# Input normalised with tokens on partitions and then transposed, parameter rows moved behind the first weight panel

## The reference

```python
def rms_norm(x, g):
    y = xf * lax.rsqrt(jnp.mean(xf * xf, axis=-1, keepdims=True) + RMS_EPS)
    return (y * g.astype(jnp.float32)).astype(x.dtype)

h = h + token_mixer(rms_norm(h, g_mix[l]), w_in[l], rnn_conv_w[l], ...)
    # inside: z = u @ w_in; split into u_rnn, u_gelu, c_val, c_gate, z_ga, z_gb
    # RG-LRU branch on u_rnn/u_gelu, 31-tap causal convolution branch on c_val/c_gate,
    # merged by sigmoid gates and projected by w_out
h = h + hierarchical_moe(rms_norm(h, g_ffn[l]), ...)
return rms_norm(h, g_final)
```

## Time and profile before

| | us |
|---|---|
| Median of 3 runs | 533.61 (533.55 to 533.82) |
| Span of the profiled execution | 531.7 |
| The profiled execution's own device time | not listed |
| TensorE busy in it | 509.5 (96%) |
| VectorE, ScalarE, GpSimd busy | 273.2, 209.2, 9.6 |
| Mean granted TensorE clock | 0.987 |

### The profile page before, as it was taken

How to read it: one execution, slowest core, us unless ns; L and a number is a source line. 1 busy time by engine, 2 the same in 40 slices (tenths; PEclk the granted TensorE clock), 3 DMA queues, 4 the chain that set the end, 5 groups by cost and what they waited for, 6 DMA issues and landing times.

```text
span 531.7 us, 8105 instructions
## 1 busy us (share of the span) xinstructions
PE 509.5 (96%) x2983; PEld 359.7 (68%) x2983; DVE 273.2 (51%) x550; ACT 209.2 (39%) x315; POOL 9.6 (2%) x25
## 2 busy tenths in 40 slices
PE   4999999999999999999989999999999999999994
PEld 4998888888999999999964353535435353534531
DVE  0589999969999996678282202221221212122123
ACT  2561113323897779345243231412323141322414
POOL 3020000000000000000000000000000000000000
PEclk8799999999999999999999999999999999999998
DMA  7594995434444438759996999999999999999932
GB/s 238 171 250 159 300 301 182 141 125 146 152 154 163 158 109 283 244 166 326 322 387 248 363 361 373 372 350 369 356 367 372 372 361 359 372 372 369 355 137 79
DMA packets 115970, 143.31 MB, mean 270 GB/s; under 512 B 3934, under 2 KB 106398, under 8 KB 115946
## 3 DMA queue, kind: packets, MB, share of 16 engines
q1 hardware_dynamic: 115502, 141.75, 79.5%
q0 software_dynamic: 432, 1.21, 0.8%
q10 hardware_dynamic: 12, 0.02, 0.0%
HBM read 141.90 MB, written 1.05 MB: 269 GB/s over the span
## 4 chain that ended last, share of the span: by engine, by line
PE 90%; DVE 4%; ACT 3%; DMA 2%; issue 1%; SPq 0%; DVEq 0%; ACTq 0%
PE ps L1267 21%; PE ps L1067 17%; PE ps L1304 11%; PE ps L1076 7%; PE ps L1078 7%; PE ps L1077 7%; PE ps L1219 6%; PE ps L1250 6%; DMA bufB<-in_conf_conv_b 2%; PE ps L1114 1%; PE ps L1109 1%; DVE ring_r L676 1%; PE ps L1032 1%; PE ps L1277 1%; PE ps L1286 1%; ACT bufC L565 1%
## 5 line engine op out<-in xcount | busy, mean ns | idle before, releaser
L1067 PE MATMUL ps<-actT,ring 128*128 128x256 f32 x416 | 90.8, 380 | 1.5 <-ACT gateA L448 1.0
L748 DVE SCALAR_TENSOR_TENSOR cacc<-cpad,par,cacc 128x256 f32<-128x256 f32 x226 | 90.3, 477 | 0.0
L1067 PEld LDWEIGHTS ps<-actT,ring 128*128 128x128 f32 x416 | 78.7, 190 | 13.1 <-ACT gateA L448 1.6
L1267 PE MATMUL ps<-ring,xslot 128*64 128x512 f32 x384 | 85.1, 594 | 0.0
L975 DVE SCALAR_TENSOR_TENSOR y_lo<-ps,wslot,y_hi 128x1024 fp32r<-128x1024 f32 x16 | 20.5, 1284 | 105.6 <-ACT y_hi L624 105.6
L1267 PEld LDWEIGHTS ps<-ring,xslot 128*64 128x64 f32 x384 | 27.0, 137 | 52.2 <-issue 51.4
L676 DVE TENSOR_TENSOR ring_r<-ring,ring_r 128x2048 fp32r<-128x2048 f32 x23 | 52.1, 2284 | 1.4 <-ACT ring_r L455 1.3
L1076 PE MATMUL ps<-u_hi,ring_r 128*128 128x256 f32 x176 | 50.4, 286 | 0.7 <-issue 0.7
L1077 PE MATMUL ps<-u_lo,ring_r 128*128 128x256 f32 x176 | 49.8, 283 | 0.0
L1078 PE MATMUL ps<-u_hi,ring_r 128*128 128x256 f32 x176 | 49.8, 283 | 0.0
L455 ACT ACTIVATE ring_r<-ring 128x2048 fp32r<-128x2048 f32 x23 | 43.7, 1907 | 8.4 <-DMA ring<-in_w_rnn_out 2.7
(11 more groups left out here) (230 smaller groups left out, 775.6 us busy)
## 6 DMA issues: line engine op xcount, KB each, us to landing
ring<-in_w_in SPq DMA_DIRECT2D x24, 1024.0 KB, 5.2
ring<-in_w_gate SPq DMA_DIRECT2D x48, 512.0 KB, 8.8
ring<-in_w_up SPq DMA_DIRECT2D x48, 512.0 KB, 8.9
ring<-in_w_down SPq DMA_DIRECT2D x40, 512.0 KB, 8.1
ring_high<-in_w_gate SPq DMA_DIRECT2D x16, 512.0 KB, 8.9
ring_high<-in_w_up SPq DMA_DIRECT2D x16, 512.0 KB, 9.0
ring_high<-in_w_down SPq DMA_DIRECT2D x16, 512.0 KB, 8.2
ring<-in_w_rnn_out SPq DMA_DIRECT2D x4, 1024.0 KB, 4.9
```

Source lines behind the costliest of these rows:

```text
L748: ins = v.scalar_tensor_tensor(out=d if k == taps - 1 else a, in0=s, scalar=w, in1=start(c) if start and k == first else a, op0=ALU.mult, ...
L1067: last = pe.matmul(ps[:, m % 4, 0:T], w[:, k, (m % 2) * P:(m % 2 + 1) * P], actT[:, k, :], start=(k == 0), stop=(k == KC - 1))
L1267: last = pe.matmul(ps[SLOTS * j:SLOTS * (j + 1), 4, :], xslot[:, k, e * SLOTS:(e + 1) * SLOTS], w, start=(k == 0), stop=(k == KC - 1), ski ...
```

## The change

Normalising now happens before the transposes, with tokens on partitions, where 1/rms is a scalar of each partition.

- ScalarE's queue first issues g_mix broadcast to all 128 partitions (`gmix`, 0.5 MB). Per tile of x: square and sum, variance, root, reciprocal, and one VectorE instruction `u_tok = x * rstd * gmix`.
- TensorE transposes `u_tok` into banks 4 to 7, two chunks to a bank. Banks 4 and 5 are copied to `actT` by ScalarE, 6 and 7 by VectorE. `u_hi` and `u_lo` are made in four pieces straight from PSUM. The diagonal product and the row `lnw` are gone.
- SP issues panel 0 before the parameter rows. TensorE transposes the rows after panel 0 (`parameter_columns`), and VectorE copies them to `par` after the low part of panel 1. g_mix's row is still loaded into `vecs`.
- `keep_warm` is 12 and 1 products where it was 7, 6 and 7. The counts of the semaphores shift with all this.

```diff
+        gmix = bufD[:, 0:4, :].rearrange("p a b -> p (a b)")
+        u_tok = bufC[:, :, :].rearrange("p (t a) b -> p t (a b)", t=TC)
@@ sync
                 sp.dma_start(hres[:, tc, :], x_v[:, tc, :]).then_inc(x_in[tc], 16)
-            for r, v in param_rows[:5]:
-                sp.dma_start(vecs[r:r + v.shape[0], :], v).then_inc(vec_in, 16)
...
                 sp.dma_start(slot_kn(ring, MIX_SLOT + k % SEG), src).then_inc(mixw_full[k % SEG], 16)
+                if k == 0:
+                    for r, v in param_rows[:5]:
+                        sp.dma_start(vecs[r:r + v.shape[0], :], v).then_inc(vec_in, 16)
@@ scalar
+            act.dma_start(gmix, bcast(g_mix, 0, P)).then_inc(gmix_in, 16)
             for r, v in param_rows[5:]:
                 act.dma_start(vecs[r:r + v.shape[0], :], v).then_inc(vec_in, 16)
...
-            act.wait_ge(dve_var, 1)
-            act.activation(stat[:, 4:6], stat[:, 2:4], ACT.Sqrt).then_inc(act_std, 1)
-
-            act.wait_ge(pe_chunk, KC)
-            act.wait_ge(par_ready, 1)
-            for c in range(KC):
-                act.activation(actT[:, c, :], ps[:, c % 4, c // 4 * T:(c // 4 + 1) * T], ACT.Copy,
-                               scale=par[:, c, R_GMIX:R_GMIX + 1]).then_inc(act_evac, 1)
+                act.wait_ge(dve_var, tc + 1)
+                act.activation(stat[:, 4 + tc:5 + tc], stat[:, 2 + tc:3 + tc], ACT.Sqrt).then_inc(act_std, 1)
+
+            for b in range(2):
+                act.wait_ge(pe_uT, b + 1)
+                act.activation(uT_pair(actT, b), ps[:, 4 + b, :], ACT.Copy).then_inc(act_uT, 1)
+            for b in range(4):
...
+                act.activation(uT_pair(u_hi, b), ps[:, 4 + b, :], ACT.Copy).then_inc(act_evac, 2)
...
-            act.wait_ge(dve_u, KC)
-            act.activation(u_hi[:, :, :], actT[:, :, :], ACT.Copy).then_inc(act_split, 1)
             for k in SPLIT[:3]:
                 weight_hi(k)
@@ vector
+            for tc in range(TC):
...
+                v.reciprocal(stat[:, 6 + tc:7 + tc], stat[:, 4 + tc:5 + tc]).then_inc(dve_rstd, 1)
+                v.wait_ge(dve_rstd, tc + 1)
+                if tc == 0:
+                    v.wait_ge(gmix_in, 16)
+                v.scalar_tensor_tensor(out=u_tok[:, tc, :], in0=hres[:, tc, :], scalar=stat[:, 6 + tc:7 + tc],
+                                       in1=gmix, op0=ALU.mult, op1=ALU.mult).then_inc(dve_utok, 1)
+            for b in (2, 3):
+                v.wait_ge(pe_uT, b + 1)
+                v.tensor_copy(uT_pair(actT, b), ps[:, 4 + b, :]).then_inc(dve_uT, 1)
+            for b in range(4):
+                v.wait_ge(act_evac, 2 * b + 2)
+                v.tensor_tensor(uT_pair(u_lo, b), ps[:, 4 + b, :], uT_pair(u_hi, b).bitcast(F32), ALU.subtract
+                                ).then_inc(dve_split, 1)
+
+            weight_lo(SPLIT[0])
             v.wait_ge(pe_par, 1)
             v.tensor_copy(par[:, :, :].rearrange("p k r -> p (k r)"), ps[:, 7, 0:KC * NROW]).then_inc(par_ready, 1)
...
-            for c in range(KC):
-                v.wait_ge(act_evac, c + 1)
-                v.tensor_tensor(actT[:, c, :], actT[:, c, :], lnw[:, 2, :], ALU.mult).then_inc(dve_u, 1)
...
-            v.wait_ge(dve_u, KC)
-            operand_lo(1, u_lo[:, :, :], actT[:, :, :], u_hi[:, :, :])
-            for k in SPLIT[:3]:
+            for k in SPLIT[1:3]:
                 weight_lo(k)
@@ tensor
-            keep_warm(7)
+            keep_warm(12, bank=3)
             for tc in range(TC):
-                pe.wait_ge(x_in[tc], 16)
+                pe.wait_ge(dve_utok, tc + 1)
                 for c in range(KC):
...
+                    last = pe.transpose(ps[:, 4 + c // 2, c % 2 * T + tc * P:c % 2 * T + (tc + 1) * P],
+                                        u_tok[:, tc, c * P:(c + 1) * P], ident[:, :])
...
-            keep_warm(6)
-
-            for tc in range(TC):
-                pe.wait_ge(dve_rdiag, tc + 1)
-                last = pe.matmul(ps[:, 6, tc * P:(tc + 1) * P], ones[:, :], rdiag[:, tc, :], start=True, stop=True)
-            last.then_inc(pe_rstd, 1)
-            keep_warm(7)
+            keep_warm(1, bank=3)
+
+            def parameter_columns():
+                pe.wait_ge(vec_in, 16 * 11)
+                pe.wait_ge(dve_split, 4)
...
             whole_panel(0, 0, first=True)
-            pe.wait_ge(dve_split, 1)
+            parameter_columns()
             for k in SPLIT[:3]:
                 split_panel(k, u_hi, u_lo, evac_bank)
```

More of the change, by code:

```diff
@@ L175, in build @@
         act_step = sem("act_step")
-        dve_rdiag = sem("dve_rdiag")
-        pe_rstd = sem("pe_rstd")
+        gmix_in = sem("gmix_in")
         dve_rstd = sem("dve_rstd")
-        dve_u = sem("dve_u")
+        dve_utok = sem("dve_utok")
+        pe_uT = sem("pe_uT")
+        act_uT = sem("act_uT")
+        dve_uT = sem("dve_uT")
         pe_par = sem("pe_par")
@@ L264, in build, with uT_pair @@
         C_HALVES = (slice(0, KC // 2), slice(KC // 2, KC))
+        def uT_pair(t, b):
+            return t[:, 2 * b:2 * b + 2, :].rearrange("p a b -> p (a b)")
         def unit(u):
@@ L1028, in _, with keep_warm @@
         def _(pe):
-            def keep_warm(n):
+            def keep_warm(n, bank=5):
                 for _ in range(n):
-                    pe.matmul(ps[:, 5, 0:P], ones[:, :], ones[:, :], start=True, stop=True)
+                    pe.matmul(ps[:, bank, 0:P], ones[:, :], ones[:, :], start=True, stop=True)
             pe.wait_ge(gp_step, 3)
-            keep_warm(7)
+            keep_warm(12, bank=3)
             for tc in range(TC):
-                pe.wait_ge(x_in[tc], 16)
+                pe.wait_ge(dve_utok, tc + 1)
                 for c in range(KC):
-                    last = pe.transpose(ps[:, c % 4, c // 4 * T + tc * P:c // 4 * T + (tc + 1) * P],
-                                        hres[:, tc, c * P:(c + 1) * P], ident[:, :])
-            last.then_inc(pe_chunk, KC)
-            pe.wait_ge(vec_in, 16 * 11)
-            for c in range(KC):
-                last = pe.transpose(ps[:, 7, c * NROW:(c + 1) * NROW], vecs[:, c * P:(c + 1) * P],
-                                    ident[0:NROW, 0:NROW])
-            last.then_inc(pe_par, 1)
-            keep_warm(6)
-            for tc in range(TC):
-                pe.wait_ge(dve_rdiag, tc + 1)
-                last = pe.matmul(ps[:, 6, tc * P:(tc + 1) * P], ones[:, :], rdiag[:, tc, :], start=True, stop=True)
-            last.then_inc(pe_rstd, 1)
-            keep_warm(7)
+                    last = pe.transpose(ps[:, 4 + c // 2, c % 2 * T + tc * P:c % 2 * T + (tc + 1) * P],
+                                        u_tok[:, tc, c * P:(c + 1) * P], ident[:, :])
+                    if tc == TC - 1 and c % 2:
+                        last.then_inc(pe_uT, 1)
+            keep_warm(1, bank=3)
+            def parameter_columns():
+                pe.wait_ge(vec_in, 16 * 11)
+                pe.wait_ge(dve_split, 4)
+                for c in range(KC):
+                    last = pe.transpose(ps[:, 7, c * NROW:(c + 1) * NROW], vecs[:, c * P:(c + 1) * P],
+                                        ident[0:NROW, 0:NROW])
+                last.then_inc(pe_par, 1)
             def whole_panel(s, p, first=False):
@@ L1061, in whole_panel @@
                 for m in (2 * p, 2 * p + 1):
-                    pe.wait_ge(act_evac, s * KC + max(KC + m - 3, KC))
+                    if not first:
+                        pe.wait_ge(act_evac, s * KC + max(KC + m - 3, KC))
                     for k in range(KC):
-                        if first:
-                            pe.wait_ge(dve_u, k + 1)
+                        if first and k % 2 == 0:
+                            pe.wait_ge(act_uT if k < 4 else dve_uT, k % 4 // 2 + 1)
                         last = pe.matmul(ps[:, m % 4, 0:T], w[:, k, (m % 2) * P:(m % 2 + 1) * P],
                                          actT[:, k, :], start=(k == 0), stop=(k == KC - 1))
-                    last.then_inc(pe_chunk, 1)
+                    last.then_inc(pe_chunk, KC + 1 if first and m == 0 else 1)
             def split_products(dst, w_hi, w_lo, x_hi, x_lo, before=None):
@@ L1127, in _ @@
                     channel_sums(bufB, 5)
[L1129 removed]
+            pe.wait_ge(dve_split, 4 + 1)
             for k in range(K_YA, K_YB):
                 split_panel(k, bufA_r, bufG_r, evac_bank)
[L1133 removed]
+            pe.wait_ge(dve_split, 4 + 3)
             def yb_bank(m):
@@ L1171, in _ @@
                                    lambda k: w_hi[:, k, :], lambda k: w_lo[:, k, :],
-                                   before=(lambda k: pe.wait_ge(dve_split, 4 + k + 1)) if p == tc == 0 else None
+                                   before=(lambda k: pe.wait_ge(dve_split, 4 + 3 + k + 1)) if p == tc == 0 else None
                                    ).then_inc(pe_wout, 1)
```

28 lines of the change are left out of this document (11 added, 17 removed).

## The result

The changed kernel takes 535.41 us (median of 8 runs, 534.89 to 536.13), the kernel before beside it 533.72 us (8 runs, 533.53 to 534.58). The ratio is 1.0025, with a 95% interval of 1.0016 to 1.0034: slower, where 532.7 us and a gain had been forecast. The profiled execution took 535.45 us at a span of 533.6 us, 1.9 us more than the 531.7 of before.

What follows compares the result with a forecast made beforehand. TensorE's matmuls bind the kernel; at the start, one DMA engine carrying parameter rows delays panel 1. −3.5 us (panel 1 earlier) + 2.6 (clock) = −0.9: span 530.8, with 1.9 added 532.7 us; 8-in-10 range 531.0 to 534.2.

Steps and rivals of the forecast that it cites:

- The steps up to the split panel: Start: panel 0 begins at 12.1, panel 1 lands at 20.6, its split matmuls begin at 25.0, 3.5 us earlier.
- The row wait: Prologue: TensorE's 10.64 us wait for a parameter row (to 13.74) was to leave it.
- its end was hidden: Panel 0: ends at 19.2; half clock would cost up to 3.5 us, hidden by the next step.
- the queue of one engine: Start: parameter rows sit on one DMA engine, panel 1 queues behind them and lands at 20.6 (20.5 to 21.3).
- the slower rival: Panel 1 not queued behind the rows, landing at 23.4; TensorE starts it at 27.8: +1.9, so 535.5 us; chance 0.11.
- The clock's term: Panel 1: matmuls at half speed for 5.1 us lose 2.6 us; bounds nothing to 3.1.
- the sum: Whole kernel: −3.5 (start of panel 1) + 2.6 (clock) = −0.9 us, span 530.8, time 532.7 us.
- so the start moves everything alike: From 46.5 on: TensorE runs without a pause, so the start's gain shifts everything later equally, with two conditions.
- two conditions: Later stages: VectorE's stream caps the gain at 2.3 us; the experts' DMA given nothing, under a tenth if lead mattered.
- a later stage that doesn't shift with the start: Changed profile: listed among the signs that would show the prediction wrong; no size given.
- the chance of 0.09 for slower: Whole kernel: chance of being slower by more than 1.07 us, all from the case of panel 1 landing late.
- The full-clock rival: Start: clock doesn't fall, or earlier; 3.5 us won at panel 1, VectorE's start allows 2.3: 531.3 us; chance 0.30.

Runs made afterwards that it cites:

- e6_rows_spread: Changed kernel with 21 instead of 12 keep-warm products at the start and the 31 rows of conf_conv_w loaded by two DMAs (16 and 15): 526.50 us.
- e2_fill_wait: Changed kernel with 3 instead of 12 keep-warm products at the start and 18 in TensorE's wait before panel 1: 531.31 us, ratio 0.9942.
- e1_pad_front: Changed kernel with 21 instead of 12 keep-warm products at the start: 532.06 us, ratio 0.9962 to the kernel before.
- e10_nine_in_wait: Changed kernel with nine keep-warm products added in TensorE's wait before the split panel, none at the start: 531.32 us, ratio 0.9952.
- e5: Changed kernel with 16 instead of 12 keep-warm products at the start: 532.43 us, ratio 0.9975.
- e4: Kernel before without nine of its keep-warm products (seven at the start, two ahead of panel 0): 536.24 us, ratio 1.0037.
- e7: Kernel before with only the 31 rows of conf_conv_w loaded by two DMAs (16 and 15 rows): 526.61 us, ratio 0.9863.
- e9: Changed kernel with only the 31 rows of conf_conv_w spread over two DMAs, 12 keep-warm products kept at the start: 529.58 us, ratio 0.9919.
- e3: Changed kernel with 12 instead of 8 keep-warm products ahead of the experts' loop: 533.52 us, ratio 0.9979.

## Why the prediction was wrong

The steps up to the split panel were right. The row wait left the prologue; panel 0 began at 13.09 (12.1 forecast) and its end was hidden, as argued; the queue of one engine set panel 1's landing at 20.9 (20.6), although SP issued the panel only at 6.82 (near 4 forecast), and the slower rival, panel 1 not queued behind the rows, did not happen. The rule of the Trainium skill, "DMA: Bandwidth & Descriptors", "Why a DMA increments its semaphore by 16 and not by 1", was weighed against the change rightly, and e6_rows_spread shows its other side: two copies of 16 and 15 rows, which by that rule run on 16 and 15 engines, took 5 us off the landing of panel 1. The trace agrees (share 1.09 instead of 0.64).

The clock's term was mis-sized upwards. 2.6 us were forecast for 5.1 us at half speed; it lasted 4.7 us, from 25.19 to 29.9, and a matmul took 0.21 us in it and not twice the 0.12 of full speed. That is 2.1 us on TensorE, and taking it away is worth 0.5 (e2_fill_wait against e1_pad_front) to 1.0 at 45 (e10_nine_in_wait against the changed kernel). With the smaller loss, the lead at 45 was 1.2 us where 0.9 stood in the sum.

The step that failed is "so the start moves everything alike", with its two conditions, VectorE's stream and the experts' DMA. Neither of these bound. The prediction named the sign itself: "a later stage that doesn't shift with the start". The sum left out that removing nine instructions moves everything that is behind them in TensorE's stream: when its instruction packets come (0.63 us) and how fast it enters the experts' loop (1.03 us, and the clock's fall behind it, 1.50 us). e1, e5 and e10 add products that compute nothing and win 3.4, 3.0 and 4.1 us (0.3, 0.5 and 1.0 of it at the start); e4 takes eight instructions' worth of place from the kernel before and loses 2.3. The prediction had no term for taking instructions out. No rival had this cost, the range ended at 534.2, and the chance of 0.09 for slower was given to another mechanism altogether: its 535.5 us is the measured time by coincidence, for panel 1 landed at 20.9 and not at 23.4. The full-clock rival gave 531.3, which e2 and e10 measured once the instructions lay at the old place (531.31 and 531.32), but what held them there at 32 us was ScalarE (TensorE waits 0.70 and 0.69 us), and not the start of VectorE's stream that the rival named.

Was the change itself good, then? With the instructions at the old place it is: e10_nine_in_wait is 2.4 us and e1_pad_front 1.9 us faster than before, against the 0.9 of the sum. But most of what it did was to step round the slow rows; two DMAs in place of one gain 7.2 us without it (e7).

What stays open: why the pause at the entry grows by degrees (1.28, 1.46, 1.75, 2.25, 2.31 us at 1380, 1375, 1373, 1372, 1371). It is TensorE's own, for VectorE's release is earlier, and it goes with place and not with the start (e9, e10). But place is not all: e7 has 1.43 us at 1380, and at 1375 TensorE follows VectorE's release after 0.4 us in e5 and after 0.2 in e3. That it is the supply of instructions is likely but not seen, since no instruction packet falls within it. Also open is when a pause lets the clock fall: 2.3 us did in the profiled run of the changed kernel, not in those of e4 and e9, and in e2 the clock stayed at 1.00 through 5.74 us without work, up to 9.25.

## What to carry to other kernels

Filler instructions are not free to remove: they also hold the place of what stands behind them. When a small edit moves a later, untouched stage, compare loop entries and the landing times of transfers there between the two traces, and put as many idle instructions back as the edit took out before judging it. And look at how a small load's rows divide over the DMA engines first: 31 rows as 16 and 15 were worth more than the whole reordering.

## What the runs showed of the hardware

- Where an instruction packet of 16 KB came 1 to 3 us behind the issue of the 1 MB transfer of `w_rnn_out`, it took 5.8 to 6.4 us (six kernels), and 4.9 to 5.3 where the packet came just ahead (six). ScalarE waits for that transfer, and TensorE lost 0.5 to 1.0 us. A packet 4.3 us behind the issue cost two other transfers nothing (5.2 us).
- In the changed kernel the granted clock rose from 1.2 to 2.4 GHz at about 12.85, when TensorE had done nothing but transposes since 9.28. In e10_nine_in_wait, with the same start of the program, it rose only at 15.09, behind the same transposes and 1.7 us of panel 0.
- VectorE's one long pause without a releaser ahead of `bufB` was 4.99 to 5.10 us in the three kernels with the old program of VectorE (before, e4, e7) and 2.7 to 3.0 in the nine with the new one. An instruction packet of 8 KB (queue q14) comes within it in all twelve, and VectorE goes on 2.35 to 2.6 us behind that packet's start each time: at 117.08 behind 114.70 in the kernel before, at 116.11 behind 113.54 in the changed one. In the old program the pause begins 2.6 to 2.7 us ahead of the packet, in the new one 0.3 to 0.4. That fits an engine that stands still until its instructions have come, sooner or later by their place in its program, though no run varied this alone. It cost nothing in the kernels at 534; in e7_before_rows_spread, whose chain runs through VectorE there, it may.
